# Second block's layer norms: lower parts and residual sums on VectorE, work on pairs of tiles, layer loops written out

## What is computed

```python
def second_block(x, p, w_in, ...):
    for i in range(DEPTH):                      # DEPTH = 2
        proj = x @ w_in[i]
        ...                                     # neighbourhood attention ya, retention yb
        merged = jax.nn.sigmoid(gate_a) * (ya @ w_branch_a[i]) + jax.nn.sigmoid(gate_b) * (yb @ w_branch_b[i])
        y = merged @ w_out[i]
        x = layer_norm(DEEPNORM_ALPHA * x + y, ln1_g[i], ln1_b[i])
        ffn = conv_glu_ffn(x, w_up[i], conv_w[i], conv_b[i], w_down[i])
        ple = jax.nn.sigmoid(x @ w_ple_gate[i]) * (p[i] @ w_ple_proj[i])
        x = layer_norm(DEEPNORM_ALPHA * x + ffn + ple, ln2_g[i], ln2_b[i])
    return x

def layer_norm(x, g, b):
    mu = jnp.mean(x, axis=-1, keepdims=True)
    var = jnp.mean(jnp.square(x - mu), axis=-1, keepdims=True)
    return (x - mu) * lax.rsqrt(var + LN_EPS) * g + b
```

## Time and profile before

| | |
|---|---|
| timed runs, median (lowest to highest) | 2057.84 us (2054.29 to 2058.98) |
| profiled execution, device time | 2051.96 us |
| its span, first to last instruction | 2050.2 us |
| mean granted TensorE clock | 0.991 |
| TensorE busy | 2007.6 us |
| VectorE busy | 1347.4 us |
| ScalarE busy | 1060.5 us |
| GpSimd busy | 195.5 us |

### The profile page before, as it was taken

How to read it: one execution, slowest core, us unless ns; L and a number is a source line. 1 busy time by engine, 2 the same in 40 slices (tenths; PEclk the granted TensorE clock), 3 DMA queues, 4 the chain that set the end, 5 groups by cost and what they waited for, 6 DMA issues and landing times.

```text
span 2050.2 us, 36130 instructions
## 1 busy us (share of the span) xinstructions
PE 2007.6 (98%) x14488; PEld 1882.6 (92%) x14488; DVE 1347.4 (66%) x1596; ACT 1060.5 (52%) x1262; POOL 195.5 (10%) x157
## 2 busy tenths in 40 slices
PE   7999999999999999999999999999998999999997
PEld 6999999999999999998999999989998999998996
DVE  6666666766676667677666755678775655557775
ACT  5444555544554455554446543466555543356654
POOL 0000130000000003000004012030006003010001
PEclk9999999999999999999999999999998999999998
DMA  6554544455455554455555444555543544544541
GB/s 261 195 184 167 190 158 165 184 184 184 168 193 184 184 184 173 155 213 185 184 184 184 167 144 165 182 186 202 184 184 124 177 153 146 186 162 168 198 184 45
DMA packets 53275, 359.91 MB, mean 176 GB/s; under 512 B 6320, under 2 KB 7728, under 8 KB 10544
## 3 DMA queue, kind: packets, MB, share of 16 engines
q1 hardware_dynamic: 49248, 350.01, 47.5%
q10 hardware_dynamic: 3328, 4.20, 0.7%
q0 software_dynamic: 592, 4.19, 0.5%
HBM read 353.14 MB, written 1.05 MB: 173 GB/s over the span
## 4 chain that ended last, share of the span: by engine, by line
PE 67%; issue 28%; POOL 2%; ACT 1%; DVE 1%; DMA 0%; SPq 0%; POOLq 0%; ACTq 0%; DVEq 0%
PE gate_two L1396 8%; PE up_two L1396 8%; PE gate_two L1361 8%; PE gate_two L1362 7%; PE gate_two L1363 7%; PE bank L1361 6%; PE bank L1363 6%; PE bank L1362 6%; PE gate_two L1398 4%; PE up_two L1398 4%; POOL br_parts L407 1%; PE bank L1473 1%; PE up_two L1504 1%; PE up_two L1488 1%; PE bank L1724 1%
## 5 line engine op out<-in xcount | busy, mean ns | idle before, releaser
L892 DVE TENSOR_TENSOR w_lo<-raw,w_hi 128x2048 fp32r<-128x2048 f32 x330 | 764.5, 2318 | 325.0 <-ACT w_hi L522 324.8
L522 ACT ACTIVATE w_hi<-raw 128x2048 fp32r<-128x2048 f32 x330 | 628.4, 1905 | 70.1 <-PE bank L1363 61.7
L1396 PE MATMUL gate_two<-br_parts,w_hi 128*128 128x512 f32 x1056 | 379.1, 401 | 15.8 <-DVE w_lo L892 15.8
L1396 PE MATMUL up_two<-br_parts,w_hi 128*128 128x512 f32 x1056 | 376.1, 399 | 0.1
L1361 PE MATMUL gate_two<-br_parts,w_hi 128*128 128x256 f32 x1152 | 334.0, 290 | 9.2 <-POOL br_parts L407 9.1
L1363 PE MATMUL gate_two<-br_parts,w_hi 128*128 128x256 f32 x1152 | 328.2, 285 | 0.0
L1362 PE MATMUL gate_two<-br_parts,w_lo 128*128 128x256 f32 x1152 | 328.2, 285 | 0.0
L1398 PE MATMUL gate_two<-br_parts,w_lo 128*128 128x256 f32 x1056 | 297.7, 282 | 0.0
L1398 PE MATMUL up_two<-br_parts,w_lo 128*128 128x256 f32 x1056 | 296.7, 281 | 0.0
L1362 PE MATMUL bank<-hid_hi,w_lo 128*128 128x256 f32 x960 | 271.9, 283 | 0.0
L1361 PE MATMUL bank<-hid_lo,w_hi 128*128 128x256 f32 x960 | 271.8, 283 | 0.0
(11 more groups left out here) (235 smaller groups left out, 3010.7 us busy)
## 6 DMA issues: line engine op xcount, KB each, us to landing
raw<-stream SPq DMA_DIRECT2D x330, 1024.0 KB, 4.8
area<-rpb POOLq DMA_DIRECT2D x2, 1536.0 KB, 7.3
softT<-area ACTq DMA_DIRECT2D x32, 64.0 KB, 4.8
konst<-consts SPq DMA_DIRECT2D x1, 1344.0 KB, 13.9
x<-xT SPq DMA_DIRECT2D x4, 256.0 KB, 4.0
area<-area ACTq DMA_DIRECT2D x8, 128.0 KB, 5.7
ret_turn<-area ACTq DMA_DIRECT2D x8, 128.0 KB, 2.5
result<-x SPq DMA_DIRECT2D x4, 256.0 KB, 2.5
```

Of the source, the lines that this page charges most:

```text
L522: act.activation(w_hi[:, s, :], raw[:, s, :], ACT.Copy).then_inc(hi_ready[s], 1)
L892: dve.tensor_tensor(w_lo[:, s, :], raw[:, s, :], w_hi[:, s, :].bitcast(F32), ALU.subtract).then_inc(lo_ready[s], 1)
L1396: pe.matmul(pair[:, f, :, :], w_hi[:, s, at:at + P], parts[:, :, k, :], start=k == 0, stop=False, skip_group_check=True)
```

## The change

Four things, all in the second block's norms except the last.

- The lower parts (br_lo) are computed by VectorE, as scaled tile + shift - upper part (shifted_lower), each behind the scaling of the next tile. The sums over pairs (pair_sum) also go to VectorE, behind the addition of the bank that completes a pair. GpSimd keeps only the power and load_tables.
- Subtraction of the mean and squaring work on pairs of tiles, with half as many instructions and semaphore steps.
- ScalarE writes all eight upper parts first and the eight tiles of x behind them; in the first norm x comes after the split of m = 37. The splits at m = 36 and at the last chunks of the layer stand earlier. In the last layer's second norm there are no upper and lower parts, since nothing reads them.
- The layer loops of ScalarE, VectorE and GpSimd are written out; cur and gain1 are no longer copied, but read in place from col1 and col2. The semaphores cur_ready and gain_ready go.

The diff, cut to its core (the rest replaces Fori by range, drops the copies, and counts c_ready and c_sq by pairs):

```diff
@@ GpSimd
             def layer_norm(here, n):
 
-                for j in (1, 2):
-                    pool.wait_ge(z_ready.sem, here.at(z_ready, HALVES * n + j + 1))
-                    if j == 2:
-                        pool.wait_ge(z_sum.sem, here.at(z_sum, 2 * n + 1))
-                    pool.tensor_tensor(z_pairs, x[:, 0:2, :] if j == 1 else z_pairs, x[:, 2 * j:2 * j + 2, :], ALU.add
-                                       ).then_inc(z_sum.sem, 1)
                 pool.wait_ge(ln_var.sem, here.at(ln_var, n + 1))
                 power(rs[:, :], ms[:, :]).then_inc(ln_rs.sem, 1)
-                for k in range(DT):
-
-                    pool.wait_ge(xs_hi.sem, here.at(xs_hi, DT * n + k + 1))
-                    rest(br_lo[:, k, :], x[:, k, :], br_hi[:, k, :]).then_inc(xs_ready.sem, 1)
-
-            with pool.Fori(0, DEPTH) as layer:
+
+            for layer in range(DEPTH):
...
                 layer_norm(here, 0)
-                with pool.If(layer < DEPTH - 1):
-                    following = nc.s_assert_within(layer + 1, 1, DEPTH - 1, skip_runtime_bounds_check_because="the If bounds it")
-                    load_tables(following, layer + 2)
+                if layer < DEPTH - 1:
+                    load_tables(layer + 1, layer + 2)
                 layer_norm(here, 1)
@@ ScalarE, second block
-            with act.Fori(0, DEPTH) as layer:
+            for layer in range(DEPTH):
                 here = Place(1, layer)
-                act.wait_ge(xs_ready.sem, here.at(xs_ready, 0))
+                cur = col2[:, layer, :]
                 split_hi(2, here.uses(2))
 
-                def layer_norm(n, col_b, spare=lambda: None):
-
+                def variance(n):
                     act.wait_ge(var_ready.sem, here.at(var_ready, n + 1))
                     act.activation(ms[:, :], banks[7][:, 0, 0:TT], ACT.Identity, bias=eps5).then_inc(ln_var.sem, 1)
-                    spare()
+
+                def shifted_upper(n, col_b):
+                    for k in range(DT):
+                        act.wait_ge(ln_scaled.sem, here.at(ln_scaled, DT * n + k + 1))
+                        act.activation(br_hi[:, k, :], work[:, k, :], ACT.Identity,
+                                       bias=cur[:, col_b + k:col_b + k + 1]).then_inc(xs_hi.sem, 1)
+
+                def shifted(n, col_b):
                     for k in range(DT):
                         act.wait_ge(ln_scaled.sem, here.at(ln_scaled, DT * n + k + 1))
                         act.activation(x[:, k, :], work[:, k, :], ACT.Identity, bias=cur[:, col_b + k:col_b + k + 1]
                                        ).then_inc(x_new.sem, 1)
-                        act.activation(br_hi[:, k, :], work[:, k, :], ACT.Identity,
-                                       bias=cur[:, col_b + k:col_b + k + 1]).then_inc(xs_hi.sem, 1)
 
                 def centred_squares(n):
-                    for k in range(DT):
-                        act.wait_ge(c_ready.sem, here.at(c_ready, DT * n + k + 1))
-                        act.activation(work[:, k, :], x[:, k, :], ACT.Square).then_inc(c_sq.sem, 1)
+                    if n == 1:
+                        act.wait_ge(x_new.sem, here.at(x_new, DT))
+                    for j in range(HALVES):
+                        act.wait_ge(c_ready.sem, here.at(c_ready, HALVES * n + j + 1))
+                        act.activation(work[:, 2 * j:2 * j + 2, :], x[:, 2 * j:2 * j + 2, :], ACT.Square
+                                       ).then_inc(c_sq.sem, 1)
...
                     elif m == 36:
-                        def ple_first():
-                            for a in range(2):
-                                e = act.activation(ple_out[:, 2 * a:2 * a + 2, :], banks[4 + a][:, :, :], ACT.Copy)
-                            e.then_inc(mix_evac.sem, 1)
-                            split_after(here, m)
-                        layer_norm(0, C_B1, ple_first)
+                        split_after(here, m)
+                        for a in range(2):
+                            e = act.activation(ple_out[:, 2 * a:2 * a + 2, :], banks[4 + a][:, :, :], ACT.Copy)
+                        e.then_inc(mix_evac.sem, 1)
+                        variance(0)
+                        shifted_upper(0, C_B1)
                     elif m == 37:
...
                         split_after(here, m)
+                        shifted(0, C_B1)
...
                         if c == CHUNKS[1] - 3:
+                            if layer < DEPTH - 1:
+                                split_after(here, c, turn)
                             hidden_upper(here, PAIRS - 1, att_hi)
...
                 centred_squares(1)
-                layer_norm(1, C_B2)
+                variance(1)
+                if layer < DEPTH - 1:
+                    shifted_upper(1, C_B2)
+                shifted(1, C_B2)
@@ VectorE, second block
                 def centred(n):
                     dve.wait_ge(mu_ready.sem, here.at(mu_ready, n + 1))
-                    for k in range(DT):
-                        dve.tensor_tensor(x[:, k, :], x[:, k, :], banks[6][:, 0, :], ALU.subtract).then_inc(c_ready.sem, 1)
-
-                def layer_norm(n, col):
+                    mu = banks[6][:, 0:1, :].broadcast_to([P, 2, T])
+                    for j in range(HALVES):
+                        two = x[:, 2 * j:2 * j + 2, :]
+                        dve.tensor_tensor(two, two, mu, ALU.subtract).then_inc(c_ready.sem, 1)
+
+                def pair_sum(n, j):
+
+                    dve.wait_ge(z_ready.sem, here.at(z_ready, HALVES * n + j + 1))
+                    if j == 2:
+                        dve.wait_ge(z_sum.sem, here.at(z_sum, 2 * n + 1))
+                    dve.tensor_tensor(z_pairs, x[:, 0:2, :] if j == 1 else z_pairs, x[:, 2 * j:2 * j + 2, :], ALU.add
+                                      ).then_inc(z_sum.sem, 1)
+
+                def layer_norm(n, col, col_b, lower=True):
+
+                    def shifted_lower(k):
+                        dve.wait_ge(xs_hi.sem, here.at(xs_hi, DT * n + k + 1))
+                        dve.scalar_tensor_tensor(out=br_lo[:, k, :], in0=work[:, k, :],
+                                                 scalar=cur[:, col_b + k:col_b + k + 1],
+                                                 in1=br_hi[:, k, :].bitcast(F32), op0=ALU.add, op1=ALU.subtract
+                                                 ).then_inc(xs_ready.sem, 1)
 
                     dve.wait_ge(ln_rstd.sem, here.at(ln_rstd, n + 1))
                     for k in range(DT):
                         dve.scalar_tensor_tensor(out=work[:, k, :], in0=x[:, k, :], scalar=cur[:, col + k:col + k + 1],
-                                                 in1=rstd_ln, op0=ALU.mult, op1=ALU.mult).then_inc(ln_scaled.sem, 1)
+                                                 in1=rstd_ln, op0=ALU.mult, op1=ALU.mult
+                                                 ).then_inc(ln_scaled.sem, 1)
+                        if lower and k >= 1:
+                            shifted_lower(k - 1)
+                    if lower:
+                        shifted_lower(DT - 1)
...
+                        if m in (33, 34):
+                            pair_sum(0, m - 32)
...
                     elif m == 36:
-                        layer_norm(0, C_G1)
                         split_after(here, m)
+                        layer_norm(0, C_G1, C_B1)
...
-                    if c < CHUNKS[1] - 3:
+                    if c < CHUNKS[1] - 3 or c == CHUNKS[1] - 3 and layer < DEPTH - 1:
                         split_after(here, c, turn)
...
+                            if j in (1, 2):
+                                pair_sum(1, j)
                 centred(1)
-
-                with dve.If(layer < DEPTH - 1):
-                    chunk_done(here, CHUNKS[1] - 3)
-                    split_after(here, CHUNKS[1] - 3)
-                layer_norm(1, C_G2)
-                with dve.If(layer < DEPTH - 1):
+                if layer < DEPTH - 1:
                     chunk_done(here, CHUNKS[1] - 2)
                     split_after(here, CHUNKS[1] - 2)
+                layer_norm(1, C_G2, C_B2, layer < DEPTH - 1)
```

63 lines of the change are left out of this document (27 added, 36 removed).

## The result

| | median us (lowest to highest, runs) |
|---|---|
| before, timed again beside it | 2054.29 (2047.55 to 2061.86, 9) |
| after | 2045.53 (2042.84 to 2050.33, 9) |

What follows compares the result with a forecast made beforehand. TensorE was taken as the bound, busy 2007.6 of 2050.2 us. The terms +1.5 - 3.0 - 0.1 - 2.3 - 2.7 = -6.6 us, off the median of 2057.84, gave 2051.2 us, range 2046 to 2056.5.

Steps and rivals of the forecast that it cites:

- Loops written out: Layer loops of ScalarE, VectorE and GpSimd: writing them out costs nothing, at most 1 us of table load per layer.
- First norm, layer 0: Second block: faster lower parts, but the earlier mask addition holds VectorE's split of chunk 37; a loss of 1.5 us.
- addition ahead of the last lower part: Rival, layer 0's first norm: GpSimd's mask addition holds VectorE's last lower part; layer 0 loses 4.6 to 6.1 us; 25%.
- First norm, layer 1: Second block, no load_tables there: lower parts on VectorE end sooner than on GpSimd; a gain of 3.0 us.
- Second norm: Between the layers: 0.1 us from sums and pairs, 2.3 us from an earlier m=0 without its stop.
- Tail: After the last matmul: without upper and lower parts the last x tile comes sooner; a gain of 2.7 us.
- nothing moves: Rival: waits return at the split of chunk 2 or the fetch of longer programs; within 2 us of before; 5%.
- ping-pong: Rival, at the norms: each lower part waits the whole round trip to ScalarE; 6.2 us slower, 2064 us; 5%.
- no hold: Rival, layer 0's first norm: the mask addition does not block VectorE; layer 0 gains 1.6, 2048.1 us in all; 20%.

Runs made afterwards that it cites:

- e1_loops: The kernel before with only the layer loops of ScalarE, VectorE and GpSimd written out; 2057.91 us, ratio 1.0010 to the kernel before.
- e3_exp: The changed kernel with one small exp per layer in the first block, so the exp table loads while ScalarE is idle; 2045.12 us, ratio 0.9955 to before.
- e7_tail: The changed kernel with the last layer's unread upper and lower parts put back; 2054.53 us, ratio 1.0005 to the kernel before.
- e9_splits: The changed kernel with only the splits of weight chunks put back in their old places; 2054.90 us, ratio 1.0013 to the kernel before.
- e8_single: The changed kernel with mean subtraction and squares tile by tile again instead of in pairs; 2044.54 us, ratio 0.9963 to the kernel before.
- e4_gp: The changed kernel with the lower parts alone put back on GpSimd; 2047.21 us, ratio 0.9967 to the kernel before.
- e2_tables: The changed kernel with GpSimd issuing load_tables(1) only after all eight x tiles of the first norm are written; 2046.79 us, ratio 0.9963 to before.
- e12_cols: The kernel of e6_warm with the variance's matmuls 128 columns wide instead of one; 2033.17 us, ratio 0.9899 to the kernel before.
- e5_pieces: The kernel of e3_exp with GpSimd's mask addition cut into six parts; 2041.18 us, ratio 0.9942 to the kernel before.
- e6_warm: The kernel of e5_pieces with TensorE multiplying unused constants in the gaps of each second norm; 2039.00 us, ratio 0.9932 to the kernel before.

## Why the prediction was right, point by point

The time, the direction and the total were right, and part of that was luck: three terms were off by over 2 us, two stages came dearer (loops by 2.4, tail by 2.2) and one cheaper (layer 1 by 2.7).

- *Loops written out, 0 predicted:* +2.4 us measured, the step that failed. I looked for a cost at TensorE's code and at the heads of the loops and gave 1 us a layer as the bound for a table load, which takes 1.28 us in the trace; the actual place was inside the first block, at an exp whose load took over its wait. Shown by e1_loops and e3_exp.
- *First norm, layer 0, +1.5:* +0.5. The mechanism came as written: lower parts in 6.9 us (7.3 taken), power held (0.4 us, 0.7 taken), addition at 1342.4, which is 1339.9 without the 2.4 us by which all is late (1338.5 to 1340.2 taken), a wait of 2.2 us for w_lo (2.8), no fall of the clock behind it. What the forecast lacked is the fall of the clock ahead of it, at the variance. It lost some 1.7 us (an estimate: 4 x 0.29 + 4 x 0.14), which don't show in the stage, as TensorE would otherwise have waited longer for the same split. The rival *addition ahead of the last lower part* is as real: it stands in the profiles of e3_exp, e7_tail and e9_splits, with 8.5, 8.2 and 5.2 us for the stage, twice above the 4.6 to 6.1 that I gave it, as the clock falls behind the wait. The changed kernel's profile escaped it by 0.46 us. Two things go with it in the profiles: the clock within the variance (3.63 us long after the change and in e8_single, with the DMA issued 1.4 us ahead of the scaling and the addition behind the lower parts; 4.46 and 4.53 us in e3_exp and e7_tail, with 2.6 us and the addition ahead), and in e9_splits the sooner landing.
- *What gave the gain:* here the account was wrong though the sum held. I credited the lower parts on VectorE (2.3 us in layer 0's first norm, 3.6 in layer 1's). In e4_gp they are worth 0.8 us in the total, which the noise of some 2 us doesn't tell from nothing; in e9_splits the moved splits are worth about 10 us with the lower parts on VectorE. My own row of a 2.67 us subtraction beside a split had said so: that hold was a cost of the split's place, and I had booked it under the subtraction.
- *First norm, layer 1, -3.0:* -5.7. e1_loops, with the old norm, has -4.0 in this stage: the profile before had lost that to the clock, 0.50 from 1808 to 1812 and 0.62 from 1820 to 1824, where e1_loops shows 1.00 throughout. What the change itself gives is at least the rest, 1.7 us, inside the bounds of 1.3 to 3.7; it may be more, as the clock was 0.57 from 1808 to 1812 after the change and 1.00 in e1_loops. I had put 1.4 us of clock on the account and should have put 4.
- *Second norm, -2.4:* -2.6, right. Its sum of small losses was off (the variance took 4.42 us for 3.77 at a fallen clock), and no wait for chunk 2 came.
- *Tail, -2.7:* from the start of the scaling to the last x it took 3.8 us for 6.6, as forecast (the earlier trace rows against x<-area at 2038.23 for 3.30 us, 0.5 us behind the scaling), but the variance took 6.2 us for 3.8 at half clock, so this profile kept 0.5 us of it. With the clock less unlucky e2_tables and e4_gp kept 1.7 and 1.9, and e12_cols 3.3.
- *The rivals "nothing moves", "ping-pong" and "no hold":* none occurred; pairs of scaling and lower part follow at 0.79 us.

Open is how often the mask addition comes ahead of the last lower part in the changed kernel. Nine runs of it lie at or below 2050.3, so most did not, while in e7_tail, which differs from it only after 2030 us, it did in perhaps seven of twelve. The two kernels were timed on different occasions, and why they differ was not settled.

## What to carry to other kernels

When a long instruction of GpSimd meets short ones of VectorE, don't look for a better moment (e2_tables): cut it into parts, and the spread of the runs goes with the cost (e5_pieces). Price where a split or a copy stands in the order before pricing which engine runs the neighbouring work, and follow which load it releases. Where the clock falls beside a busy TensorE, look at how narrow its matmuls are; widening them by unread columns can be nearly free (0.1 us for each variance in e12_cols).

## What the runs showed of the hardware that was not expected

- A table load of 1.28 us is put ahead of the exp's own wait or takes it over, depending on how the loop around it is written: before, the exp starts 1.36 us behind the end of the load, when VectorE is done; after, the load starts when VectorE is done, and the exp 1.30 us later. A small exp in idle time takes the load off the path (e3_exp).
- GpSimd's power costs 0.70 us for the variance's 128x2 (2.67 us for the 128x2 numbers of the retention, which lie apart), 1.64 us for 128x8 and 41.4 us for 128x256; a subtraction of 128x256 takes 0.74.
- A row of the variance's float32 matmuls with 128x128 weights takes 0.113 us at full clock with one column and 0.117 with 128 (32 rows in the profile for the 16 matmuls of the program).
- Filled gaps alone did not hold the clock at 1.00 (e6_warm 0.994 in the mean, 0.70 and 0.60 at the norms); filled gaps with the variance 128 columns wide did (0.999).
